# Forget logits and rotated latent key with both weight parts side by side: 16 products in place of 24

## The reference

```python
# block 1: forgetting attention; the logits have 8 columns, one for each head
fq, fk, fv, f_logit, sq, sk, sv, g_fox, g_sb = split_columns(h @ w_in[i])
log_f = jax.nn.log_sigmoid((f_logit + forget_bias[i]).astype(jnp.float32))
...
# block 2: latent attention; the key part that is rotated has 32 columns, shared by all heads
hy_in, z_hy, c_q, c_kv, k_rope, z_attn, gate_hy, gate_attn = jnp.split(proj, split_at, axis=-1)
...
k = jnp.concatenate([k_nope, k_r], axis=-1)
k = rms_norm_2(k, g_kn[l])
k = jnp.concatenate([k[..., :QK_NOPE], rotary(k[..., QK_NOPE:], cos, sin)], axis=-1)
```

## Time and profile before

| what | value |
|---|---|
| median of 3 runs | 1698.82 us (1698.30 to 1698.88) |
| the profiled execution, its own time | 1698.62 us |
| its span | 1696.5 us |
| TensorE matmul busy | 1683.4 us, 99% of the span |
| TensorE weight load busy | 1375.3 us, 81% |
| VectorE busy | 1031.8 us, 61% |
| GpSimd busy | 716.1 us, 42% |
| ScalarE busy | 642.0 us, 38% |
| granted TensorE clock, mean | 0.999 |

### The profile page before, as it was taken

How to read it: one execution, slowest core, us unless ns; L and a number is a source line. 1 busy time by engine, 2 the same in 40 slices (tenths; PEclk the granted TensorE clock), 3 DMA queues, 4 the chain that set the end, 5 groups by cost and what they waited for, 6 DMA issues and landing times.

```text
span 1696.5 us, 21151 instructions
## 1 busy us (share of the span) xinstructions
PE 1683.4 (99%) x7666; PEld 1375.3 (81%) x7666; DVE 1031.8 (61%) x1220; ACT 642.0 (38%) x899; POOL 716.1 (42%) x303
## 2 busy tenths in 40 slices
PE   9999999999999999999999999999999999999999
PEld 7887888887788888888888888888777668888887
DVE  6767576527665456458665557786564753969451
ACT  5222222235665656321322322213545754343221
POOL 3444344444343431344444444444355433444443
PEclk9999999999999999999999999999999999999999
DMA  5332233325211221242433232332252023233243
GB/s 195 101 109 92 76 100 99 115 72 194 87 63 63 90 73 38 75 136 91 136 99 110 89 98 90 112 101 89 94 186 75 26 88 130 93 100 99 91 144 113
DMA packets 42815, 171.04 MB, mean 101 GB/s; under 512 B 4937, under 2 KB 5065, under 8 KB 41452
## 3 DMA queue, kind: packets, MB, share of 16 engines
q1 hardware_dynamic: 38736, 148.13, 26.9%
q10 hardware_dynamic: 3996, 21.73, 3.6%
HBM read 159.22 MB, written 10.62 MB: 100 GB/s over the span
## 4 chain that ended last, share of the span: by engine, by line
PE 68%; issue 21%; POOL 6%; DVE 2%; ACT 1%; DMA 0%; POOLq 0%; SPq 0%; DVEq 0%; ACTq 0%
PE psum L306 20%; PE psum L308 20%; PE psum L307 20%; POOL wlo L272 6%; PE psum L1200 1%; PE psum L1213 1%; PE psum L1744 1%; PE psum L1721 1%; PE psum L751 1%; PE psum L736 0%; DMA raw<-wk_dram 0%; PE psum L722 0%; PE psum L1190 0%; DVE psum L444 0%; PE psum L1693 0%
## 5 line engine op out<-in xcount | busy, mean ns | idle before, releaser
L272 POOL TENSOR_TENSOR wlo<-raw,whi 128x1024 fp32r<-128x1024 f32 (+2 forms) x258 | 663.8, 2573 | 893.2 <-ACT whi L294 892.7
L294 ACT ACTIVATE whi<-raw 128x1024 fp32r<-128x1024 f32 (+2 forms) x259 | 286.1, 1105 | 706.6 <-PE psum L308 696.5
L306 PE MATMUL psum<-h_hi,whi 128*128 128x512 f32 x1360 | 537.1, 395 | 2.7 <-POOL wlo L272 1.8
L308 PE MATMUL psum<-h_hi,wlo 128*128 128x512 f32 x1360 | 529.7, 389 | 0.0
L307 PE MATMUL psum<-h_lo,whi 128*128 128x512 f32 x1360 | 529.6, 389 | 0.0
L306 PEld LDWEIGHTS psum<-h_hi,whi 128*128 128x128 f32 x1360 | 255.4, 188 | 63.6 <-POOL wlo L272 4.7
L307 PEld LDWEIGHTS psum<-h_lo,whi 128*128 128x128 f32 x1360 | 255.4, 188 | 53.5 <-issue 2.2
L308 PEld LDWEIGHTS psum<-h_hi,wlo 128*128 128x128 f32 x1360 | 255.3, 188 | 53.5
L306 PE MATMUL psum<-mid_hi,whi 128*128 128x512 f32 x352 | 137.2, 390 | 0.0
L308 PE MATMUL psum<-mid_hi,wlo 128*128 128x512 f32 x352 | 137.0, 389 | 0.0
L307 PE MATMUL psum<-mid_lo,whi 128*128 128x512 f32 x352 | 136.9, 389 | 0.0
(11 more groups left out here) (387 smaller groups left out, 2395.8 us busy)
## 6 DMA issues: line engine op xcount, KB each, us to landing
raw<-wk_dram SPq DMA_DIRECT2D x220, 512.0 KB, 3.5
raw<-wd_dram SPq DMA_DIRECT2D x32, 704.0 KB, 4.1
raw<-wp_dram SPq DMA_DIRECT2D x8, 640.0 KB, 3.8
x_scratch<-xT ACTq DMA_DIRECT2D x2, 2048.0 KB, 8.9
spectra_scratch<-spec_out ACTq DMA_DIRECT2D x4, 1024.0 KB, 5.9
xT<-x_scratch ACTq DMA_DIRECT2D x8, 512.0 KB, 4.5
spec<-spectra_scratch ACTq DMA_DIRECT2D x2, 2048.0 KB, 10.2
xT<-x_dram SPq DMA_DIRECT2D x4, 512.0 KB, 7.6
```

The source lines that it names most:

```text
L272: pool.tensor_tensor(wlo[s][:, 0:w], raw[s][:, 0:w], whi[s][:, 0:w].bitcast(F32), ALU.subtract).then_inc(lo_ready, 1)
L294: act.activation(whi[s][:, 0:w], raw[s][:, 0:w], ACT.Copy).then_inc(hi_ready, 1)
L306: pe.matmul(dst, s_hi, m_hi, start=start and i == 0, stop=False, **kw)
L308: last = pe.matmul(dst, s_lo, m_hi, start=False, stop=stop and i == n - 1, **kw)
```

## The change

In the two narrow units only 64 of the 128 columns carry something that is needed. GpSimd now overwrites the other 64 columns of each chunk of `whi` with the low part of these weights (`split_lo_within`, 128 x 8 x 64 elements), in place of a whole `wlo`. TensorE runs each chunk twice, against the high and the low part of the activations (`linear_narrow`): 16 products for a unit. The result then has the sum over the high weights in one half of the rows and the sum over the low weights in the other half. VectorE moves one half beside the other and adds. For the forget logits the high part is in columns 0 to 63, and the sum is copied to the other 64 rows. For the key part the low part is in columns 0 to 63. The product of the low parts, which was left out before, is now in the sum.

```diff
+        NARROW = {BASE["fox_f"]: HD, BASE["mla_kr"]: 0}
+
+        def split_lo_within(pool, u):
+            s, a = u % 2, NARROW[u]
+            src, dst = (m[:, 0:D].rearrange("p (k c) -> p k c", c=P)[:, :, a:a + HD] for m in (raw[s], whi[s]))
+            pool.wait_ge(hi_ready, u + 1)
+            pool.tensor_tensor(dst, src, dst.bitcast(F32), ALU.subtract).then_inc(lo_ready, 1)
+
+        def linear_narrow(pe, dst, u):
+            s = u % 2
+            for c in range(DT):
+                both = whi[s][:, c * P:(c + 1) * P]
+                pe.matmul(dst, both, h_hi[:, c, :], start=c == 0, stop=False)
+                last = pe.matmul(dst, both, h_lo[:, c, :], start=False, stop=c == DT - 1)
+            last.then_inc(unit_done, 1)
+
         def stream_lo(pool, first, last):
+            for u in sorted(NARROW):
+                if first <= u < last:
+                    stream_lo(pool, first, u)
+                    split_lo_within(pool, u)
+                    first = u + 1
...
                         pe.wait_ge(lo_ready, u + 1)
-                        linear(pe, bank(6), u, h_hi, h_lo, DT)
+                        linear_narrow(pe, bank(6), u)
...
             def vector_logits(self, dve):
                 dve.wait_ge(unit_done, BASE["fox_f"] + 1)
                 dve.wait_ge(constr_ready, 1)
-                dve.tensor_scalar(prob[:, 0, :], bank(6), col("forget_bias"), None, ALU.add).then_inc(self.forget, 1)
+                high, low = slice(0, HD), slice(HD, P)
+                dve.tensor_copy(prob[high, 1, :], bank(6)[low, :]).then_inc(self.forget, 1)
+                dve.wait_ge(self.forget, 1)
+                dve.scalar_tensor_tensor(prob[high, 0, :], bank(6)[high, :], col("forget_bias", p=HD), prob[high, 1, :],
+                                         ALU.add, ALU.add).then_inc(self.forget, 1)
+                dve.wait_ge(self.forget, 2)
+                dve.tensor_copy(prob[low, 0, :], prob[high, 0, :]).then_inc(self.forget, 1)
...
-                    linear(pe, bank(j), u + j, h_hi, h_lo, DT, chunk_ready=norm_block2.ready if j == 0 else None,
-                           ready_base=norm_block2.base)
+                    if j == 5:
+                        linear_narrow(pe, bank(j), u + j)
...
-                    act.wait_ge(self.turn, 8)
-                    act.activation(sq_k[HD:QKD, :], bank(5)[HD:QKD, :], ACT.Square).then_inc(self.square, 1)
+                    act.wait_ge(self.turn, 9)
+                    act.activation(sq_k[HD:QKD, :], kr32[HD:QKD, :], ACT.Square).then_inc(self.square, 1)
...
                 dve.wait_ge(self.turn, 2)
-                dve.tensor_tensor(k_turn[HD:P, :], bank(5)[HD:P, :], tab_k[HD:P, :], ALU.mult).then_inc(self.turn, 1)
+                dve.tensor_copy(k_shift[HD:P, :], bank(5)[0:HD, :]).then_inc(self.turn, 1)
                 dve.wait_ge(self.turn, 8)
+                dve.tensor_tensor(kr32[HD:P, :], k_shift[HD:P, :], bank(5)[HD:P, :], ALU.add).then_inc(self.turn, 1)
+                dve.wait_ge(self.turn, 9)
+                dve.tensor_tensor(k_turn[HD:P, :], kr32[HD:P, :], tab_k[HD:P, :], ALU.mult).then_inc(self.turn, 1)
+                dve.wait_ge(self.turn, 10)
                 dve.tensor_copy(k_shift[low, :], k_turn[high, :]).then_inc(self.turn, 1)
...
     krp[:, 64:96], krp[:, 96:112], krp[:, 112:128] = kr, kr[:, 16:32], kr[:, 0:16]
+    krp[:, 0:64] = krp[:, 64:128]
```

More of the change, by code:

```diff
@@ L206, in build @@
         lat_factor = [rstd, at(102, "lat_factor", [P, T])]
+        kr32 = mprob[1][:, 0, :]
         tab_k, k_turn, k_shift = (at(a, f"k_part{a}", [P, T]) for a in (98, 100, 104))
@@ L758, in tensor @@
                 pe.wait_ge(foxp.ready, 32)
-                pe.wait_ge(foxp.forget, 11)
+                pe.wait_ge(foxp.forget, 13)
                 pe.wait_ge(foxp.softplus, 7)
@@ L986, in scalar @@
                 split_hi_to(act, BASE["fox_v"] + 4)
-                act.wait_ge(self.forget, 7)
+                act.wait_ge(self.forget, 9)
                 act.wait_ge(filters.stored, 32)
@@ L1080, in vector_split_sums @@
             def vector_split_sums(self, dve):
-                dve.wait_ge(self.forget, 4)
+                dve.wait_ge(self.forget, 6)
                 dve.tensor_scalar(forgets[:, :], probT[1][:, :], -1.0, None, ALU.mult).then_inc(self.forget, 1)
-                dve.wait_ge(self.forget, 5)
+                dve.wait_ge(self.forget, 7)
                 for rows in (slice(32, 64), slice(96, 128)):
@@ L1086, in vector_split_sums @@
                                              ALU.mult, ALU.subtract).then_inc(self.forget, 1)
-                dve.wait_ge(self.forget, 7)
+                dve.wait_ge(self.forget, 9)
         foxp = FoxProjections()
@@ L1621, in tensor_latents @@
                         pe.wait_ge(filters.spec, 32)
-                    linear(pe, bank(j), u + j, h_hi, h_lo, DT, chunk_ready=norm_block2.ready if j == 0 else None,
-                           ready_base=norm_block2.base)
+                    if j == 5:
+                        linear_narrow(pe, bank(j), u + j)
+                    else:
+                        linear(pe, bank(j), u + j, h_hi, h_lo, DT, chunk_ready=norm_block2.ready if j == 0 else None,
+                               ready_base=norm_block2.base)
                     if j == 3:
@@ L1667, in tensor_v @@
                     pe.wait_ge(self.factor, 4)
-                    pe.wait_ge(self.turn, 13)
+                    pe.wait_ge(self.turn, 15)
                 for t in range(first, first + 2):
@@ L2113, in pool_key_rotated @@
                 else:
-                    pool.wait_ge(self.turn, 13)
+                    pool.wait_ge(self.turn, 15)
                 pool.wait_ge(self.q_lo, h + 1)
```

14 lines of the change are left out of this document (7 added, 7 removed).

## The result

| | before | the change |
|---|---|---|
| median of 8 executions each | 1698.72 us | 1705.02 us |
| lowest to highest | 1698.30 to 1698.88 | 1702.37 to 1708.58 |
| profiled execution, its span | 1698.62, 1696.5 | 1704.05, 1702.3 |

The ratio is 1.0039, with a 95% interval of 1.003 to 1.0047: the change is slower by 6.3 us, outside the predicted range. The kernel does less and takes longer, and it varies by 6 us where before varied by 0.6. The executions differ in TensorE's mean granted clock: the two with 1.000 took 1702.4 us, those from 0.997 to 0.999 took 1704.05 to 1706.94, and the one with 0.946 took 1708.6. So there is a fixed loss, and one that comes and goes.

The account below looks back on a forecast made before the run. TensorE's matmuls, filling 99% of the span, were taken to bound the kernel. From the profiled 1698.62 us, -1.46 at k1 and +0.70 at the latents, -0.76 together, gave 1697.9 us; range 1695.6 to 1699.7.

Parts of the forecast that it names:

- The failed step: Fox projections: VectorE's logits grow to three operations, 1.2 us more, up to 3; priced at nothing, 1 us if uncovered.
- a cover of 0.72 us: VectorE's idle time right behind the forget logits, 0.72 us, taken to absorb part of the added logits work.
- the clock rival: TensorE's clock falls in the wait for k0: 1703.3 us, or 1700.6 with half of k0 slow; chance 0.05.
- k0 fixed at 405.55 with a wait of two microseconds: Behind `fox_f`, k0's start does not move, so the 1.81 us saved there are lost waiting for GpSimd.
- 16 products in 3.63 us: Each narrow unit, `fox_f` and `mla_kr`, runs 16 products on TensorE and is 3.63 us long.
- k1's gain of 1.46: Fox projections: k1's low part is ready earlier, so k1 starts at 411.65 instead of 413.11, gaining 1.46 us.
- The latents, +0.70 net: TensorE gains 1.07 us at z0, then loses it and 0.70 more at z2, behind VectorE's held-up key chain.
- The sum: Whole kernel: -1.46 at k1 plus 0.70 at the latents, -0.76 us, giving 1697.9 us.

Follow-up runs that it names:

- e13: The changed kernel, with only GpSimd's subtractions for k5 and the first three value units made to wait for VectorE's copies: 1698.28 us.
- e5: The kernel before, 24 products kept, with forget logits in three VectorE operations all reading PSUM, the first only 8 columns wide: 1703.92 us.
- e7: The changed kernel with the three logits operations behind the first query tile in place of the second: 1699.49 us.
- e2: The kernel before with only the key unit (latents) changed, the forget unit left as before: 1699.09 us.
- e11: e2 with two compressed-key latents ahead of the key chain on VectorE, and z0's weight split ahead of ScalarE's second latent: 1696.71 us.
- e3: The kernel before, 24 products kept, with only the forget logits made three VectorE operations, the last a copy in SBUF: 1704.71 us.
- e9: The changed kernel with logits and VectorE's minimum-and-subtract one tile earlier, and eight extra products in the wait for k0: 1697.92 us.
- e10: e5 with VectorE's minimum-and-subtract and the memset behind it one tile earlier: 1698.62 us.

## Why the prediction was wrong

- **The failed step**: "VectorE's logits grow from one operation to three [...] I price it at nothing, and at 1 us if that cover is gone". It is worth 1702.4 - 1697.9 = 4.5 us (the change at full clock, less e13 at full clock). I asked how late the added work made the next tile, set a cover of 0.72 us against it, and bounded the rest by its own length. The last copy met GpSimd, as the text allowed (1.95 us), and so 2.7 us were added; but e5 shows that as little as 0.27 us beyond the cover costs 3.4 us and more, because the order of GpSimd's subtraction and VectorE's operations turns over and each later pair of copies is held up by 2.1 us. The same prediction followed such hold-ups step by step in the latents, and did not ask at the fox projections which VectorE operations GpSimd now starts ahead of; the two rows that tell it (L1071 at 433.11, GpSimd at 433.33) stood in the timelines of before.
- **The second step**: the clock rival at 0.05. Its mechanism is as described, and its size smaller than priced: 2.7 us for half of k0 at the low clock; in the profile after, k0 takes 7.19 us to the sum of squares behind it, against 5.58 in e13's, so 1.6, and e13's slower group is 1.7 above the other. Its chance was too low by far: of e13's eleven executions five show it, and of e7's ten at least the five between 1699.4 and 1699.8. The row used for it, a clock that held over the gap ahead of k1, was a gap of under a microsecond.
- **k0 fixed at 405.55 with a wait of two microseconds**: right (405.43, 2.24). **16 products in 3.63 us**: right in both places.
- **k1's gain of 1.46**: right as a mechanism (k1's low part was ready at 410.36, forecast 410.7), taken back here by the low clock. In e13's profile, with the clock at 1.00, k1 starts at 411.76 (forecast 411.65).
- **The latents, +0.70 net**: right in kind, too large. Measured 0.3 in the profile and 0.5 in e2; z2 waited 1.53 against the 1.7 forecast. In e2's profile L1973's successor starts at 1267.64, forecast 1267.95. The copy out of PSUM took 0.68 us and was not held up, as assumed. The remedy that follows from it, latents first, gave 2.4 us (e11 against e2).
- **The sum** -0.76 would have been right without the failed step and the fall of the clock: 1697.9 was forecast, and e13's executions at full clock are at 1697.8 to 1698.3.

## What to carry to other kernels

Where GpSimd and VectorE both work from SBUF in a loop, look for the pairs of operations that start within half a microsecond of each other, and ask of every edit, however well covered, whether it changes their order: here 0.27 us beyond the cover was enough. The price is then not the edit's length but nearly GpSimd's whole operation, once a turn for as long as the meeting lasts. A gate that makes GpSimd wait for VectorE's short copies cost nothing that could be measured here and makes the order certain. A product saved in front of a wait was no gain here, and in some executions a loss, since TensorE stood still longer and its clock fell.

## What was not expected of the hardware

- A meeting of VectorE and GpSimd that keeps itself up: 2.1 us lost at each pair of copies of the fourth, fifth and sixth tile, since every later step is delayed alike. The Trainium skill (SBUF — State Buffer, Who interferes with whom) says that the order of issue, and not the kind of operation, decides which of the two is blocked, for the whole instruction. The rows agree: L1071 0.22 ahead of GpSimd cost GpSimd 0.35 us (2.75 in place of 2.40), the same operation 0.04 behind it took 2.90 in place of 0.69.
- TensorE's clock fell to 0.54 behind a standstill of 2.24 us (profile after) and stayed at 1.00 behind one of 2.38 us (profile of e13, same place). Behind the 3.32 us at the second value unit it fell in e3's profile (0.76 from 452 to 456) and stayed at 1.00 in the profile after. Whether it falls differs from one execution to the next, and the length of the standstill alone does not tell. The Trainium skill (TensorE: Matmul & The Clock Gate, What's actually happening) calls the count of slow products at a kernel's start variable from run to run. The groups of e7 and e13 show the same of a fall in the middle of a kernel.
- A copy out of PSUM was not held up by GpSimd: in e11 VectorE's L2023 took 0.68 us at 1259.49, between two GpSimd operations of which one always ran.

Left open: which operations meet in e9's two long executions, since its profile is of a short one; and why both times of before, 1698.5 and 1699.4, occur at full clock. A hint is in e10's profile, which is of an execution of the longer kind (1699.47, 24 products): GpSimd's subtraction for `fox_f` starts at 397.15 and takes 2.93 us, VectorE's sum beside it takes 0.68, and TensorE waits 1.19 us for the unit; in the profile of before the sum took 2.72, the subtraction 2.39, and the wait was 0.47. The two start 0.01 us apart in e10's profile and 0.22 in that of before, so there too which of them goes first may decide.
